# Memory heads first: the order of head pairs in two attention layers of a four-layer kernel

## The chip, the cores and the metric

The kernel runs on one core of a Trainium2 chip. The time is device time in microseconds (us) of one launch. Five engines work side by side, each through its own queue in order: TensorE (PE; its weight loads are listed as PEld), VectorE (DVE), ScalarE (ACT), GpSimd (POOL) and SyncE (SP, which issues the loads). They meet at semaphores.

## What is computed

Two blocks of two layers each. The first block (sliding-window attention with a state-space mixer, then sparse attention) is untouched by the change. In the second block each layer has 12 mixing heads and 4 heads that attend to 256 memory tokens, all 64 wide, over 512 positions; a gated feed-forward network with a short convolution follows. Cut to what matters:

```python
for layer in range(DEPTH):
    xn, mn = rmsnorm(h, norm_mix[layer]), rmsnorm(mem, norm_mem[layer])
    if kind == 0:                      # layer 0: causal, decay by forget gates
        q, k, v, f_logit, qm = jnp.split(xn @ w_in_fox[slot], ...)
        mix = fox_attention(q, k, v, log_sigmoid(f_logit + b_forget))
    else:                              # layer 1: rotary positions, dilated windows
        q, k, v, qm = jnp.split(xn @ w_in_dil[slot], ...)
        mix = dilated_attention(apply_rope(q), apply_rope(k), v)
    mem_out = memory_attention(qm, mn, w_mem_kv[layer])   # softmax(qm km^T / 8) vm
    h = h + merge_heads(concatenate([mix, mem_out])) @ w_out[layer]
    h = h + conv_ffn(rmsnorm(h, norm_ffn[layer]), ...)
```

## The kernel before

All is in fp32. A dense product is made exact enough by splitting both factors into a high and a low part and adding three products (`product`, line 488). The weights come in slots, in the order in which they are listed at lines 419 to 430: SyncE loads a slot, ScalarE or GpSimd copies the high part and GpSimd subtracts for the low part, both on 128x512 pieces, and TensorE uses it. Three slots are kept split at a time; GpSimd begins with the next when TensorE has used up the oldest.

The class `Mixer` (line 2336 on) does attention for one layer. Its heads go in pairs: pairs 0 to 5 are mixing heads, `m0` and `m1` are memory heads. `SEQ` gives the order of the pairs, and each pair has four steps, one for each block `qb` of 128 query rows, so 32 steps. One step is a small pipeline for two heads `e`:

- TensorE `scores`: queries times keys into PSUM bank 0 or 1 (line 2513), in layer 0 with the decay added by a second product from `cum` (line 2521). A mixing pair has 128 (qb + 1) keys, a memory pair always 256. Two steps often share a bank, then the scores of both are issued with the first.
- VectorE `logits`: mask and scale, with a row statistic (line 2676). ScalarE `probs`: exp, with its row sum (line 2630). VectorE `scaled`: reciprocal and multiplication (lines 2685, 2686).
- TensorE `turn`: transposes into banks 2 and 3 (line 2533). ScalarE `copy` brings them to SBUF (line 2640). After a pair's four steps TensorE `values` multiplies with the values into bank 4 (line 2548), and VectorE `finish` splits the result.

Between steps TensorE is fed with the dense products that make the queries, keys and values of later pairs. They are listed as blocks in `self.blocks`, each with its weight slot, kind and bank: "turned" blocks are 512 wide and put queries or keys by head dimension, "tokens" blocks are 256 wide and put values by position. Blocks ahead of `self.prelude` are made before the first step: the first two blocks of queries (banks 4, 5) and of keys (banks 6, 7), in layer 0 the forget gates (bank 0), and the values of pairs 0 and 1, four tiles in banks 1 to 4. The rest stands in `self.fill` and goes between steps, a tokens block or half a turned block in one step, all in banks 6 and 7. ScalarE `evacuate` copies a finished block out of its bank (line 2622). A block may only begin when the block before it in the same bank has been copied.

In layer 1 queries and keys get rotary positions: ScalarE `swap` copies halves crosswise to bank 5 (line 2600), VectorE `rope` multiplies and adds (lines 2700 to 2703). The four tiles of the first pairs are done ahead of the first `logits` on VectorE's queue. In layer 0 VectorE makes the running sum `cum` of the forget gates (lines 2708 to 2717) ahead of it.

TensorE's queue at a start, as the code has it:

```python
for m in range(4, self.prelude):
    self.dense(pe, m, 0, KD)
if layer == 0:
    self.dense(pe, *self.fill[0])
scores(0)
if layer == 1:
    self.dense(pe, *self.fill[0])
for s in range(self.N):
    if s + 1 < self.N:
        scores(s + 1)
    if s + 1 < len(self.fill):
        self.dense(pe, *self.fill[s + 1])
    ...
    turn(s)
```

Of the kernel before, what the change touches and what calls it, by code (L numbers as in the profile page):

```python
# [28 lines left out]
T = S // P  # L29
# [13 lines left out]
FH, FD = 12, 64  # L43
# [298 lines left out]
def block_kernel(nc, t, out):  # L342
    ctx = ExitStack()
    with ctx:
# [8 lines left out]
        def wide(w, c0, width, kd=KD):  # L353

            first = len(W.slots)
            for c in range(c0, c0 + width, 256):
                n = min(256, c0 + width - c)
                W.add(kd, n, [(0, tiles(w, 0, kd)[:, :, c:c + n])])
            return first
# [11 lines left out]
        AW, CW, FW = AH * AD, CH * CD, FH * FD  # L371
# [35 lines left out]
        w_mem_k, w_mem_v, w_q, w_k, w_v, w_qm, w_out = ([0, 0] for _ in range(7))  # L407
# [6 lines left out]
        for layer in range(2):  # L414
            w_in = (fox, dil)[layer]
            w_q[layer], w_k[layer], w_v[layer] = [0] * 3, [0] * 3, [0] * 3
            w_q[layer][0] = wide(w_in, 0, 256)
            w_k[layer][0] = wide(w_in, FW, 256)
            if layer == 0:

                w_forget = wide(w_in, 3 * FW, P)
            w_v[layer][0] = wide(w_in, 2 * FW, 256)
            w_qm[layer] = wide(w_in, 3 * FW + (FH if layer == 0 else 0), 256)
            for i in range(1, 3):
                w_q[layer][i] = wide(w_in, 256 * i, 256)
                w_k[layer][i] = wide(w_in, FW + 256 * i, 256)
                w_v[layer][i] = wide(w_in, 2 * FW + 256 * i, 256)
            w_out[layer] = deep(t["w_out_2"][layer], 0, KD)
            for part, (u0, units) in enumerate(PARTS):
                w_up[layer, part] = len(W.slots)  # L430
                down = tiles(t["w_down_2"][layer], u0, units)
                quarters = {f"{odd + 1}{half + 1}": down[:, odd::2, half * 512:half * 512 + 512] for odd in range(2) for half in range(2)}
                up = tiles(t["w_up_2"][layer], 0, KD)
                for i in range(u0, u0 + units):
                    if i == u0 + units - 2:
                        arrived_12 = W.add_first_quarter(units // 2, quarters["12"])
                    W.add(KD, 256, [(0, up[:, :, i * P:(i + 1) * P]), (P, up[:, :, DFF + i * P:DFF + (i + 1) * P])], i >= SPLIT, part > 0 and i == u0)
                w_down[layer, part] = W.add_group(units // 2, quarters, arrived_12)
# [1899 lines left out]
        class Mixer:  # L2338

            SEQ = (0, 1, "m0", "m1", 2, 3, 4, 5)
            N = 8 * T

            def __init__(self, layer):
# [27 lines left out]
                wq, wk, wv, wqm = w_q[layer], w_k[layer], w_v[layer], w_qm[layer]  # L2373
# [3 lines left out]
                        b.append((slot, "turned", j, bank + j, dst[:, j, :]))  # L2377
                if layer == 0:
                    b.append((w_forget, "forget", 0, 0, None))
                for tile in range(T):  # L2380
                    b.append((wv[0], "tokens", tile, 1 + tile, self.v[:, tile, 0:256]))
                self.prelude = len(b)
                self.first_v = self.prelude - T

                def turned(slot, dst, j0):
                    for j in range(2):
                        b.append((slot, "turned", j, 6 + j, dst[:, j0 + j, :]))

                def tokens(slot, i):
                    for tile in range(T):  # L2390
                        b.append((slot, "tokens", tile, 6 + tile % 2, self.v[:, tile, 256 * i:256 * i + 256]))
                turned(wqm, self.qm, 0)
                turned(wq[1], q_, 2)
                turned(wk[1], k_, 2)
                tokens(wv[1], 1)
# [88 lines left out]
            def tensor(self, pe):  # L2484
                layer, out_ = self.layer, self.out

                def scores(s):
                    i, p, qb = self.steps[s]
                    if self.column(p, qb):
                        return  # L2490
                    if qb == 0:
                        if isinstance(p, str):
                            j = int(p[1])
                            pe.wait_ge(self.evacuated.s, self.evacuated.at(self.made[w_qm[layer], j] + 1))
                            pe.wait_ge(memory.evacuated, 4 * layer + 4)
                        elif layer == 0:
                            pe.wait_ge(self.evacuated.s, self.evacuated.at(self.made[w_k[layer][p // 2], p % 2] + 1))
                        else:
                            place = [(id(d), tile) for d, tile, _ in self.rope_tiles].index((id(self.k), p))
                            pe.wait_ge(self.roped, place + 1)  # L2500
                    if s == 0:
                        pe.wait_ge(self.evacuated.s, self.evacuated.at(self.first_v + 1))
                        if layer == 0:
                            pe.wait_ge(self.cum_ready, 1)
                    else:
                        pe.wait_ge(self.logged.s, self.logged.at(2 * s))
                    decay = layer == 0 and not isinstance(p, str)
                    blocks = (qb, qb + 1) if qb < T - 1 and self.column(p, qb + 1) else (qb,)
                    for b in blocks:
                        c, w = self.column(p, b), self.keys(p, b) * P  # L2510
                        for e in range(2):
                            q_, k_, _ = self.head(p, e)
                            mm = pe.matmul(ps[:, e, c:c + w], q_[:, b * P:(b + 1) * P], k_[:, 0:w], start=b == qb, stop=not decay,  # L2513
                                           skip_group_check=True)
                            if not decay:
                                mm.then_inc(self.scored.s, 1)
                    for b in blocks if decay else ():
                        c, w = self.column(p, b), self.keys(p, b) * P
                        for e in range(2):
                            hd = 2 * p + e  # L2520
                            pe.matmul(ps[:, e, c:c + w], self.sel[:, hd:hd + 1].to_broadcast([LO + FH, P]), self.cum[:, 0:w],  # L2521
                                      start=False, stop=True, skip_group_check=True).then_inc(self.scored.s, 1)

                def turn(s):
                    _, p, qb = self.steps[s]
                    if s == 0:
                        pe.wait_ge(self.evacuated.s, self.evacuated.at(self.first_v + 3))
                    for e in range(2):
                        pe.wait_ge(self.scaled.s, self.scaled.at(2 * s + e + 1))
                        if s >= 1:  # L2530
                            pe.wait_ge(self.copied.s, self.copied.at(2 * (s - 1) + e + 1))
                        for i in range(self.keys(p, qb)):
                            mm = pe.transpose(ps[:, 2 + e, i * P:(i + 1) * P], self.L[:, (2 * s + e) % 4, i * P:(i + 1) * P], ident[:, :])  # L2533
                        mm.then_inc(self.turned.s, 1)
# [58 lines left out]
            def scalar(self, act):  # L2593
                link = linker(act, act_link)

                def swap(i, x):
                    if i >= 1:
                        act.wait_ge(self.swap_free, i)
                    for q in range(4):
                        ins = act.activation(ps[32 * q:32 * q + 32, 5, :], x[32 * (q ^ 1):32 * (q ^ 1) + 32, :], ACT.Copy,  # L2600
                                             scale=1.0 if q % 2 else -1.0)
                    ins.then_inc(self.swapped, 1)
# [21 lines left out]
                def probs(s):  # L2624
                    _, p, qb = self.steps[s]
                    w = self.keys(p, qb) * P
                    for e in range(2):
                        u = (2 * s + e) % 4
                        act.wait_ge(self.logged.s, self.logged.at(2 * s + e + 1))
                        act.activation(self.L[:, u, 0:w], self.L[:, u, 0:w], ACT.Exp, scale=-1.0, bias=self.stat[:, u, 0:1],  # L2630
                                       accum_out=self.stat[:, u, 1:2]).then_inc(self.expd.s, 1)
# [11 lines left out]
                for m in range(self.prelude):  # L2643
                    evacuate(m)
                    if self.layer == 1 and 1 <= m < 5:
                        dst, tile, made = self.rope_tiles[m - 1]
                        act.wait_ge(self.evacuated.s, self.evacuated.at(max(made, 1) + 1))
                        swap(m - 1, dst[:, tile, :])
                probs(0)
                for s in range(self.N):  # L2650
                    if s + 1 < self.N:
# [648 lines left out]
```

## Time and profile before

| | us |
|---|---|
| median of 3 runs | 1711.88 |
| lowest, highest | 1711.48, 1712.64 |
| profiled execution | 1711.19 |
| its span | 1709.4 |
| TensorE busy | 1690.3 (99%) |
| VectorE busy | 1085.2 (63%) |
| GpSimd busy | 915.5 (54%) |
| ScalarE busy | 755.4 (44%) |

The profile is one execution of the program. The mixer of layer 0 lies between about 556 and 740 us, that of layer 1 between about 1136 and 1324 us. TensorE is pipelined: a matmul's record is longer than the distance to the next one's start, so what a group of matmuls costs is read from start to start. "Idle before" in square brackets is the time that the engine sat idle ahead of an instruction, and the arrow names what ended it.

### The profile page before, as it was taken

The numbers are of one execution on the slowest core, as the hardware profiler recorded it, in microseconds if no ns is written. First come the engines' busy times: TensorE is split into PE (matmuls) and PEld (weight loads), VectorE is DVE, ScalarE is ACT, GpSimd is POOL, SyncE is SP. The second block draws the span as 40 slices with busy tenths as digits, with TensorE's granted clock in tenths as the row PEclk, the third lists the DMA queues.
The fourth block names the chain that finished last, engine by engine and source line by source line (L and its number), as shares of the span: only waits on it lengthen the run. The fifth ranks groups of instructions, "written<-read, shape, count | busy, mean of one in ns | idle before, by whom it ended". The sixth has DMA issues, their size and how long they took to land.

```text
span 1709.4 us, 24809 instructions
## 1 busy us (share of the span) xinstructions
PE 1690.3 (99%) x9396; PEld 1368.5 (80%) x9396; DVE 1085.2 (63%) x2179; ACT 755.4 (44%) x1604; POOL 915.5 (54%) x839
## 2 busy tenths in 40 slices
PE   9989999999999999999999999999999999999998
PEld 7866788787689977779888888898777887888886
DVE  6987734796652355534766856866875358477478
ACT  4625523313433344424444444546664345344445
POOL 8524457463347733345654655657344563574474
PEclk9999999999999999999999999999999999999999
DMA  6320323221333321123244144142111323413421
GB/s 187 111 81 24 119 81 105 75 87 62 81 99 96 115 74 50 50 63 95 66 124 123 50 126 121 49 148 97 53 50 50 93 87 105 137 61 102 145 69 55
DMA packets 175102, 152.40 MB, mean 89 GB/s; under 512 B 6224, under 2 KB 149968, under 8 KB 174984
## 3 DMA queue, kind: packets, MB, share of 16 engines
q1 hardware_dynamic: 173384, 149.33, 28.7%
q10 hardware_dynamic: 1600, 1.48, 0.3%
q8 instruction: 75, 1.23, 0.3%
q14 instruction: 43, 0.35, 0.1%
HBM read 147.61 MB, written 2.14 MB: 88 GB/s over the span
## 4 chain that ended last, share of the span: by engine, by line
PE 93%; DVE 4%; ACT 2%; issue 1%; DVEq 0%; ACTq 0%
PE ps L488 77%; PE ps L2513 2%; PE ps L2548 2%; PE ps L2533 2%; PE ps L1970 1%; PE ps L559 1%; PE ps L1948 1%; PE ps L2521 1%; PE ps L1878 1%; PE ps L1041 1%; PE ps L1960 0%; PE ps L1887 0%; PE ps L1048 0%; PE ps L1080 0%; PE ps L991 0%
## 5 line engine op out<-in xcount | busy, mean ns | idle before, releaser
L488 PE MATMUL ps<-x_hi,w_hi 128*128 128x512 f32 (+2 forms) x1432 | 532.2, 372 | 1.0 <-ACT a_gate L1256 0.5
L488 PE MATMUL ps<-x_hi,w_lo 128*128 128x512 f32 (+2 forms) x1432 | 522.5, 365 | 0.0
L488 PE MATMUL ps<-x_lo,w_hi 128*128 128x512 f32 (+2 forms) x1432 | 522.0, 365 | 0.0
L233 POOL TENSOR_SCALAR w_hi<-w_raw 128x512 fp32r<-128x512 f32 x272 | 168.3, 644 | 498.3 <-PE ps L488 477.4
L237 POOL TENSOR_TENSOR w_lo<-w_raw,w_hi 128x512 fp32r<-128x512 f32 x272 | 360.7, 1356 | 5.9
L488 PEld LDWEIGHTS ps<-x_hi,w_hi 128*128 128x128 f32 (+1 forms) x1432 | 269.4, 188 | 60.8 <-issue 16.3
L488 PEld LDWEIGHTS ps<-x_hi,w_lo 128*128 128x128 f32 (+1 forms) x1432 | 269.3, 188 | 44.0
L488 PEld LDWEIGHTS ps<-x_lo,w_hi 128*128 128x128 f32 (+1 forms) x1432 | 269.6, 188 | 40.5
L205 POOL TENSOR_TENSOR w_lo<-w_raw,w_hi 128x512 fp32r<-128x512 f32 x158 | 212.6, 1380 | 139.6 <-ACT w_hi L189 135.8
L2989 DVE SCALAR_TENSOR_TENSOR ffn_cv<-ps,col,ffn_cv 128x510 f32<-128x510 f32 (+1 forms) x176 | 131.8, 749 | 151.9 <-ACT ffn_cv L2933 147.2
L488 PE MATMUL ps<-w_hi,ffn_a_hi 128*128 128x512 f32 x308 | 121.4, 394 | 0.8 <-DVE ffn_a_lo L3010 0.7
L2933 ACT ACTIVATE ffn_cv<-ps,col 128x512 f32<-128x512 f32 x88 | 63.6, 774 | 132.3 <-PE ps L488 132.3
L488 PE MATMUL ps<-w_hi,ffn_a_lo 128*128 128x512 f32 x308 | 120.0, 390 | 0.0
L488 PE MATMUL ps<-w_lo,ffn_a_hi 128*128 128x512 f32 x308 | 120.0, 389 | 0.0
L2630 ACT ACTIVATE mix_L<-mix_L,mix_stat 128x256 f32<-128x256 f32 (+3 forms) x128 | 69.3, 545 | 72.2 <-DVE mix_stat L2676 72.2
L488 PE MATMUL ps<-w_hi,x_hi 128*128 128x256 f32 (+1 forms) x288 | 89.8, 312 | 0.0
L488 PE MATMUL ps<-w_lo,x_hi 128*128 128x256 f32 (+1 forms) x288 | 88.3, 306 | 0.0
L488 PE MATMUL ps<-w_hi,x_lo 128*128 128x256 f32 (+1 forms) x288 | 88.2, 306 | 0.0
L205 POOL TENSOR_TENSOR w_lo<-w_chain,w_hi 128x512 fp32r<-128x512 f32 x44 | 58.8, 1368 | 47.9 <-ACT w_hi L330 47.9
L2686 DVE TENSOR_SCALAR mix_L<-mix_L,mix_stat 128x256 f32<-128x256 f32 (+3 forms) x128 | 80.2, 626 | 4.5
L189 ACT ACTIVATE w_hi<-w_raw 128x512 fp32r<-128x512 f32 x136 | 74.4, 624 | 17.6 <-PE ps L488 14.8
L516 DVE TENSOR_TENSOR h<-h,ps 128x512 f32<-128x512 f32 x32 | 21.8, 687 | 93.8 <-PE ps L488 93.8
(421 smaller groups left out, 2997.9 us busy)
## 6 DMA issues: line engine op xcount, KB each, us to landing
w_raw<-w_up SPq DMA_DIRECT2D x80, 512.0 KB, 5.2
w_raw<-od_w_in SPq DMA_DIRECT2D x12, 1024.0 KB, 5.2
w_raw<-w_in_fox SPq DMA_DIRECT2D x10, 1024.0 KB, 5.4
w_raw<-w_in_dil SPq DMA_DIRECT2D x10, 1024.0 KB, 5.0
w_raw<-w_out SPq DMA_DIRECT2D x8, 1024.0 KB, 5.0
w_raw<-w_down SPq DMA_DIRECT2D x8, 1024.0 KB, 4.9
w_raw<-ev_w_in SPq DMA_DIRECT2D x6, 1024.0 KB, 5.5
w_third<-w_down SPq DMA_DIRECT2D x18, 256.0 KB, 5.2
```

The source lines that it names most:

```text
L189: act.activation(hi, self.piece(r, i), ACT.Copy).then_inc(self.hi_by_act, 1)
L205: ins = pool.tensor_tensor(lo[:, c], self.piece(buffer, i), hi[:, c].bitcast(F32), ALU.subtract)
L233: ins = pool.tensor_scalar(hi[:, c:min(c + PIECE, size)], raw[:, c:min(c + PIECE, size)], 1.0, 1.0, ALU.mult, ALU.mult)
L237: ins = pool.tensor_tensor(lo[:, c:min(c + PIECE, size)], raw[:, c:min(c + PIECE, size)], hi[:, c:min(c + PIECE, size)].bitcast(F32), ALU. ...
L488: mm = pe.matmul(o, l, r, start=start and i == 0, stop=stop and i == 2, skip_group_check=again)
L2513: mm = pe.matmul(ps[:, e, c:c + w], q_[:, b * P:(b + 1) * P], k_[:, 0:w], start=b == qb, stop=not decay, skip_group_check=True)
L2533: mm = pe.transpose(ps[:, 2 + e, i * P:(i + 1) * P], self.L[:, (2 * s + e) % 4, i * P:(i + 1) * P], ident[:, :])
L2548: mm = pe.matmul(ps[64 * e:64 * e + 64, 4, a:S], self.head(p, e)[2](kb), self.PT[:, e, kb, a:S], start=kb == 0, stop=kb == kt - 1, skip_gr ...
L2630: act.activation(self.L[:, u, 0:w], self.L[:, u, 0:w], ACT.Exp, scale=-1.0, bias=self.stat[:, u, 0:1], accum_out=self.stat[:, u, 1:2]).the ...
L2686: dve.tensor_scalar(self.L[:, u, 0:w], self.L[:, u, 0:w], self.stat[:, u, 2:3], None, ALU.mult).then_inc(self.scaled.s, 1)
L2933: act.activation(cv[:, u % 4, half, :], ps[:, self.up_bank(u, half), :], ACT.Identity, scale=self.tap(2, half, u), bias=self.tap(3, half, ...
L2989: ins = dve.scalar_tensor_tensor(o, ps[:, self.up_bank(u, half), 0:S - back], self.tap(j, half, u), o, ALU.mult, ALU.add)
```

## The change

The order of the pairs becomes `m0, m1, 0, 1, 2, 3, 4, 5` in both layers. The two blocks of the memory heads' queries move ahead of the steps, in banks 6 and 7, and the four tiles of the first values move from there (and from banks 1 to 4) into the fill, in banks 6 and 7. The two weight slots change places. The wait of the first scores is rewritten for the new blocks, the wait of the first transposes on the value tiles goes, and ScalarE copies the fill's first block, which is now a whole values tile, ahead of the first exp.

```diff
-            w_v[layer][0] = wide(w_in, 2 * FW, 256)
             w_qm[layer] = wide(w_in, 3 * FW + (FH if layer == 0 else 0), 256)
+            w_v[layer][0] = wide(w_in, 2 * FW, 256)
...
-            SEQ = (0, 1, "m0", "m1", 2, 3, 4, 5)
+            SEQ = ("m0", "m1", 0, 1, 2, 3, 4, 5)
...
-                for tile in range(T):
-                    b.append((wv[0], "tokens", tile, 1 + tile, self.v[:, tile, 0:256]))
-                self.prelude = len(b)
-                self.first_v = self.prelude - T
...
                 turned(wqm, self.qm, 0)
+                self.prelude = len(b)
+                tokens(wv[0], 0)
                 turned(wq[1], q_, 2)
...
                     if s == 0:
-                        pe.wait_ge(self.evacuated.s, self.evacuated.at(self.first_v + 1))
+                        pe.wait_ge(self.evacuated.s, self.evacuated.at(5))
...
                 def turn(s):
                     _, p, qb = self.steps[s]
-                    if s == 0:
-                        pe.wait_ge(self.evacuated.s, self.evacuated.at(self.first_v + 3))
...
+                evacuate(self.fill[0][0])
                 probs(0)
```

What stands on ScalarE's queue at the start of layer 1, from the first dense block of the prelude on. `mix1_v` are values, `mix1_qm` the memory heads' queries, `mix1_k` a key tile whose halves are swapped, `mix1_L` the logits that exp works on. Before:

```order
L2622 ACTIVATE mix1_v_167<-ps 128x256 [waits mix_block]
L2600 ACTIVATE ps<-mix1_k_166 32x512 [waits swap_free,mix_evacuated]
L2600 ACTIVATE ps<-mix1_k_166 32x512 x3
L2622 ACTIVATE mix1_v_167<-ps 128x256 [waits mix_block] x2
L2622 ACTIVATE mix1_v_167<-ps 128x256 [waits w_used]
L2630 ACT_TABLE_LOAD
L2630 ACTIVATE mix1_L_174,mix1_stat_175<-mix1_L_174,mix1_stat_175 128x128 [waits mix_logits] x2
L2630 ACTIVATE mix1_L_174,mix1_stat_175<-mix1_L_174,mix1_stat_175 128x256 [waits mix_logits] x2
```

And in the changed kernel, whose lines have numbers that are 4 smaller there:

```order
L2618 ACTIVATE mix1_qm_168<-ps 128x512 [waits mix_block]
L2596 ACTIVATE ps<-mix1_k_166 32x512 [waits swap_free,mix_evacuated]
L2596 ACTIVATE ps<-mix1_k_166 32x512 x3
L2618 ACTIVATE mix1_qm_168<-ps 128x512 [waits w_used]
L2618 ACTIVATE mix1_v_167<-ps 128x256 [waits mix_block]
L2626 ACT_TABLE_LOAD
L2626 ACTIVATE mix1_L_174,mix1_stat_175<-mix1_L_174,mix1_stat_175 128x256 [waits mix_logits] x4
L2618 ACTIVATE mix1_v_167<-ps 128x256 [waits mix_block]
```

Ahead of the table load that goes with the first exp stand two copies of queries and one of values, where four copies of values stood; the next values tile is copied behind the exps of two steps.

On TensorE's queue the same place in layer 1, only the instructions that wait (each dense block has 24 matmuls, each half block 12; `km` are the memory keys). Before:

```order
L488 MATMUL ps<-w_hi,x_hi 128x256 [waits w_split_done]
L488 MATMUL ps<-w_hi,x_hi 128x256 [waits mix_evacuated]
L2513 MATMUL ps<-mix_k,mix_q 128x128 [waits mix_evacuated,roped]
L488 MATMUL ps<-x_hi,w_hi 128x512 [waits mix_evacuated,w_split_done]
L2533 MATMUL ps<-ident,mix_L 128x128 [waits mix_scaled,mix_evacuated]
```

In the changed kernel:

```order
L488 MATMUL ps<-x_hi,w_hi 128x512 [waits mix_evacuated,w_split_done]
L488 MATMUL ps<-x_hi,w_hi 128x512 [waits mix_evacuated]
L2511 MATMUL ps<-km_127,mix_qm 128x256 [waits mix_evacuated,mem_evacuated]
L488 MATMUL ps<-w_hi,x_hi 128x256 [waits mix_evacuated,w_split_done]
L488 MATMUL ps<-w_hi,x_hi 128x256 [waits mix_evacuated]
L2529 MATMUL ps<-ident,mix_L 128x128 [waits mix_scaled]
L2529 MATMUL ps<-ident,mix_L 128x128 [waits mix_scaled]
L2511 MATMUL ps<-km_127,mix_qm 128x256 [waits mix_logits]
```

The first dense block of the prelude, which waited for its weights alone, now waits for a copy (`mix_evacuated`) as well; the first scores no longer wait for the rotated keys (`roped`); between the first scores and the first transposes stand two tiles of values instead of two halves of a query block.

## Rows read from the trace of the kernel before

**Rows 1.** The page: busy times, and the chain by line.
```profile
PE 1690.3 (99%) x9396; PEld 1368.5 (80%) x9396; DVE 1085.2 (63%) x2179; ACT 755.4 (44%) x1604; POOL 915.5 (54%) x839
...
PE ps L488 77%; PE ps L2513 2%; PE ps L2548 2%; PE ps L2533 2%; PE ps L1970 1%; PE ps L559 1%; PE ps L1948 1%; PE ps L2521 1%; PE ps L1878 1%; PE ps L1041 1%; PE ps L1960 0%; PE ps L1887 0%; PE ps L1048 0%; PE ps L1080 0%; PE ps L991 0%
```

**Rows 2.** TensorE's waits: us in total, times, longest us.
```profile
PE ps L1016 <- DVE s_tmp L1581: 4.9, 1, 4.9
...
PE ps L2513 <- DVE mix_stat L2676: 0.4, 1, 0.4
```

**Rows 3.** Timeline, TensorE, layer 1: start, length, engine, line, operation, tiles.
```profile
1170.63 0.50 PE L488 MATMUL ps<-x_hi,w_hi 128*128 128x512 f32 x1
...
1176.22 0.38 PE L2533 MATMUL ps<-ident,mix_L 128*128 128x128 f32 x2
1176.53 0.92 PE L2513 MATMUL ps<-mix_k,mix_q 64*128 64x384 f32 x4
```

**Rows 4.** Timeline, ScalarE, layer 1.
```profile
1158.36 0.60 ACT L2622 ACTIVATE mix_k<-ps 128x512 f32<-128x512 f32 x1 [2.24 <-PE ps L488]
...
1169.88 0.38 ACT L2622 ACTIVATE mix_v<-ps 128x256 f32<-128x256 f32 x1 [1.46 <-PE ps L488]
1170.28 1.28 ACT L2630 ACT_TABLE_LOAD   x1
1171.59 0.40 ACT L2630 ACTIVATE mix_L<-mix_L,mix_stat 128x128 f32<-128x128 f32 x1
...
1174.02 0.51 ACT L2630 ACTIVATE mix_L<-mix_L,mix_stat 128x256 f32<-128x256 f32 x1 [1.55 <-DVE mix_stat L2676]
```

**Rows 5.** Timeline, VectorE and GpSimd, layer 1.
```profile
1173.66 5.13 POOL L237 TENSOR_TENSOR w_lo<-w_raw,w_hi 128x512 fp32r<-128x512 f32 x4
...
1174.86 1.50 DVE L2686 TENSOR_SCALAR mix_L<-mix_L,mix_stat 128x256 f32<-128x256 f32 x1
...
1176.46 1.17 DVE L2686 TENSOR_SCALAR mix_L<-mix_L,mix_stat 128x256 f32<-128x256 f32 x1
...
1221.25 0.35 DVE L2686 TENSOR_SCALAR mix_L<-mix_L,mix_stat 128x256 f32<-128x256 f32 x1
```

**Rows 6.** TensorE by stretch: length, busy (x), granted clock, DMA share, GB/s.
```profile
1158.25:1169.77 11.52, 11.52 (x97) 1.00 0.27 91
...
572.34:577.81 5.47, 5.47 (x27) 1.00 0.39 108
...
596.32:597.25 0.93, 0.58 (x3) 1.00 0.07 18
...
1227.09:1230.13 3.04, 3.04 (x27) 1.00 0.00 0
1219.31:1222.17 2.86, 2.86 (x15) 1.00 0.00 0
...
1204.51:1205.57 1.06, 1.06 (x9) 1.00 0.00 0
```

**Rows 7.** Timeline, start of layer 0, three engines.
```profile
589.91 1.67 DVE L2717 TENSOR_TENSOR cum<-cum,cum 12x512 fp32r<-12x512 f32 x1
593.89 5.01 POOL L237 TENSOR_TENSOR w_lo<-w_raw,w_hi 128x512 fp32r<-128x512 f32 x4
595.37 1.14 DVE L2686 TENSOR_SCALAR mix_L<-mix_L,mix_stat 128x128 f32<-128x128 f32 x1
596.43 0.41 DVE L2676 CUSTOM_DVE_ANT_0 mix_L<-ps,causal 128x256 f32<-128x256 f32 x1
597.25 0.92 PE L2513 MATMUL ps<-mix_k,mix_q 64*128 64x384 f32 x4 [0.35 <-DVE mix_stat L2676]
```

**Rows 8.** TensorE by stretch, behind its longest wait.
```profile
108.00:110.00 2.00, 1.72 (x8) 0.50 0.93 268
...
108.00:114.00 6.00, 5.72 (x36) 0.60 0.52 172
```

**Rows 9.** Timeline, TensorE's weight loads, layer 1, behind a memory pair's values.
```profile
1232.00 0.42 PEld L2533 LDWEIGHTS ps<-ident,mix_L 128*128 128x128 f32 x4 [0.81 <-DVE mix_L L2686]
```

More of the change, by code:

```diff
@@ L421, in block_kernel @@
                 w_forget = wide(w_in, 3 * FW, P)
+            w_qm[layer] = wide(w_in, 3 * FW + (FH if layer == 0 else 0), 256)
             w_v[layer][0] = wide(w_in, 2 * FW, 256)
-            w_qm[layer] = wide(w_in, 3 * FW + (FH if layer == 0 else 0), 256)
             for i in range(1, 3):
```

## The prediction, made before the changed kernel was run

> **What bounds the kernel now.** I read the page's busy times and the chain that ended last first: TensorE is busy 99% of the span, and of the chain 77% of the span lie in the one line that all its dense products share [rows 1]. A change here pays only by what it does to TensorE's own queue: it can take a wait of that engine away or add one. The list of TensorE's waits is then the budget for a gain. Its longest entries belong to the first block, and of the two layers with memory heads it holds one wait of 0.4 us [rows 2]. The timeline is sharper, because a matmul's modelled end hides a short gap: in layer 0 the first transposes start at 596.32 and the next scores at 597.25, 0.93 us later, where the same two transposes in layer 1 take from 1176.22 to 1176.53, 0.31 us [rows 3, 6, 7]. So 0.62 us are lost at the start of layer 0, and nothing is at the start of layer 1, where fills, transposes and scores follow without a gap. Little is there to be won. I therefore looked at what the change puts in front of TensorE at the two starts.
>
> **Work that only moves.** Both orders issue the same matmuls. The prelude loses four value tiles, 11.52 us, and gets two blocks of the memory queries, twice the forget block's 5.47 us, 10.94 us [rows 6]. The fill between steps changes the other way: a values tile takes 3.04 us from start to start behind another fill, half a query block 2.86 us [rows 6], so four fills cost about 0.6 us more (0.18 x 4 is 0.7). Gain and loss cancel; I count zero, at most 0.2 us either way. The scores, transposes and value products come in another order at the same price. Loads and weight splits keep their shape and their places in the queues of SP and GpSimd (the two swapped weight slots have one size). The memory keys that the first scores now need are made in an earlier stage. All this costs nothing.
>
> **Layer 1, first new wait: the bank.** Value tile 0 went to bank 1, which was free. The query block goes to bank 6, which still holds the first half of the keys. Both halves of the keys end together at 1158.25, where the value tiles now start [rows 3]; ScalarE copies the first half from 1158.36 for 0.60 us [rows 4]. TensorE can begin at 1159.02: +0.77 us. The second half is copied while the first query block runs, 5.47 us: no wait. In layer 0 the forget block lies between and covers both copies, so nothing is added there.
>
> **Layer 1, second new wait: exp behind a values tile.** This is the term that decides. ScalarE works in order. Before, its last copy of the prelude ends and its table load begins at 1170.28, and the first exp runs at 1171.59, while TensorE has two whole fills, 1170.63 to 1176.22, before it wants a transposed result [rows 3, 4]. Now ScalarE must first copy value tile 0, and TensorE makes that tile only behind the first scores. Step by step: query blocks end at 1159.02 + 10.94 = 1169.96; scores of two memory steps take 1.06 us [rows 6], to 1171.02; tile 0 ends 2.88 us (a quarter of 11.52) later, 1173.90. The copy starts 0.11 later, the load 0.40 after that, exp 1.31 after the load began, all as in [rows 4]: exp starts at 1175.72 and not at 1171.6. From a 256-wide exp's start to the start of its scaling it was 0.84 us (1174.02 to 1174.86 [rows 4, 5]), so the first scaling begins at 1176.56. GpSimd is then in the middle of the subtractions that end at 1178.79 [rows 5]. Scalings of this width take 0.35 us beside an idle GpSimd and 1.17 to 1.50 us beside these subtractions [rows 5]; the one that began at 1176.46 ended at 1177.63. I take that row for the first and the end of GpSimd's batch for the second, 1178.9. The next logits take 0.82 us until TensorE may overwrite their bank (596.43 to 597.25 [rows 7]), so the third step's scores start at 1179.7. TensorE alone would be there at 1176.78 (second fill) + 0.62 (four transposes, twice the 0.31) = 1177.4. Wait: 2.3 us. With no contention the scalings end at 1176.9 and 1177.45, the scores start at 1178.3, and the wait is 0.9 us. Layer 1 costs 0.77 + 2.3 = 3.1 us, with ends at 1.7 and, should the batch stand 0.8 us later, 4.0.
>
> The Trainium skill, GPSIMD Engine Reference, section Key points, says that GpSimd shares its SBUF interfaces with VectorE, with contention for VectorE instructions in a two-port mode or with two SBUF inputs. By that rule the scaling suffers and the logits, which read PSUM, don't. The trace agrees: the 128x256 logits took 0.41 us inside GpSimd's batch [rows 7].
>
> **Layer 0.** The fill of tile 0 already stands ahead of the first scores, so the copy is early: forget ends at 577.81, 10.94 + 2.88 later it is 591.63. The running sum of the forget gates is ready at 591.58 [rows 7]: no wait, but no margin. The exp table is loaded 0.5 us after the tile, to 593.47, just as the first logits are ready (scores 1.06 us, logits 0.41 us). The first scaling falls at 594.3, again into the GpSimd batch from 593.89 to 598.90, as before [rows 7]. So both scalings end where they ended, the second at 596.51, and the next scores start at 597.25 again. But TensorE has less to do until then: 591.63 + 1.06 + 2.88 + 0.62 = 596.19. The wait is 1.06 us where it was 0.62: +0.4 us, from -0.6 (no contention) to +1.8 (one subtraction more, 5.01 / 4 = 1.25 us).
>
> **Later steps.** In layer 1 the rope tiles of the second queries and keys now fall beside the second memory pair and pair 0. A memory pair needs half as many value products, and every second memory step has no scores, so VectorE has less cover in steps 5 to 9; in return the later ropes get more. Before, TensorE's weight loads waited 0.81 us once behind a memory pair's values [rows 9], and its matmuls not at all by the list. I add 0.2 us, between -0.3 and +1.
>
> **The sum.** 3.1 + 0.4 + 0.2 = +3.7 us. The profiled execution took 1711.19 us (its span is 1709.4, 1.8 lie around it), so it would take 1714.9; the median of three is 1711.88, so I predict 1715.6.
>
> **Rivals.** *The scalings miss GpSimd's batch.* The price falls to 1.7 in layer 1 and to about -0.6 in layer 0; with one of the four scalings still caught it is more: +1.1 to +2.9, time 1713.0 to 1714.8. For it: the batch's position moves with every rope before it. Against it: the batch starts at 1173.66, behind a batch that GpSimd finishes without waiting, and the change leaves those alone. It decides from where the two scalings together wait less than 1.5 us. This one is not slower by the bound.
> *The clock.* After the longest wait of the kernel, 4.9 us, the granted clock was 0.50, the lower of its two levels (1.2 against 2.4 GHz), and over the 6 us from 108 to 114 it averaged 0.60 [rows 2, 8]: 6 x 0.40 = 2.4 us lost. If layer 1's waits (0.8 before the first scaled tile, 1.3 before the second, the rest ahead of the scores) bring that about, the time is 1711.9 + 3.7 + 2.4 = 1718.0. Against it: transposes lie between, and the 0.62 us of layer 0 left the clock at 1.00 [rows 6]. The Trainium skill, TensorE: Matmul & The Clock Gate, section Part 1: The HAM clock gate, says that an idle array falls to half clock; by that rule, too, the total wait would have to be one stretch.
> *The ropes are the gain.* If TensorE loses more beside ropes than starts show, say the 0.81 us [rows 9] and as much again in steps that I can't see, and the table load is hidden after all, the change saves 1.5 to 2 us: 1710. To be faster by 3.4 us it would need more idle time than both layers have.
> That the change does something else than it says is ruled out by the order of instructions.
>
> **Chances.** Forecast, +3.0 to +4.8: 0.56, of which 0.45 lie above 3.4 us. Missed batch: 0.27. Clock or a like addition: 0.08. Ropes: 0.09, of which 0.04 faster. A measurement of this kernel can tell about 0.2%, 3.4 us, from no change; the forecast lies just above it. Slower 0.45 + 0.08 = 0.53, same 0.11 + 0.27 + 0.05 = 0.43, faster 0.04. The range takes in the missed batch and the clock: 1713.0 to 1718.1 (rounded out).
>
> **What would show it.** In the profile after: in layer 1 a TensorE gap of 0.7 to 0.8 us between the key block and the queries' block; ScalarE's copy of a values tile and the table load ahead of layer 1's first exp, which runs about 4.1 us later than before; first transposes of layer 1 waiting on the scaling, then scores waiting on the logits, together 2.3 us; scalings of 1.1 to 1.3 us there; in layer 0 the same scores at 597.25. I am wrong if exp runs before the values copy, if the scalings take 0.35 us, or if the waits are there and the span does not grow by their sum, which would mean that gaps I did not see were closed elsewhere.

## The result, and the profile after

The changed kernel is slower: a median of 1717.49 us (1716.89 to 1718.48) against 1712.03 us for the kernel before on the same chip, a ratio of 1.0031 with a 95% interval of 1.0020 to 1.0042. That is +5.5 us, where 1715.6 us, +3.7, had been forecast; the range, up to 1718.1, held it. The profiled execution took 1717.48 us, its span is 1715.7 (before 1709.4).

TensorE's busy time on the page is the same as in [rows 1] to 0.1 us, so no work came on; it waits more. Engine, busy us, share, instructions:

```profile
PE 1690.4 (99%) x9396; PEld 1368.5 (80%) x9396; DVE 1082.4 (63%) x2179; ACT 755.8 (44%) x1604; POOL 917.9 (53%) x839
```

The list of TensorE's waits in layer 1 (1136 to 1324 us), where before there was none (us in total, times, longest):

```profile
PE ps L2529 <- DVE mix_L L2683: 1.3, 2, 0.8
PE ps L488 <- ACT mix_k L2618: 0.8, 1, 0.8
PE ps L2511 <- DVE mix_stat L2673: 0.7, 3, 0.3
PE ps L2529 <- ACT mix_PT L2636: 0.3, 1, 0.3
```

The timeline of TensorE shows the places. The first row is the query block that waits for its bank, then come the first scores, the transposes of the first step (two and two) and the third step's scores, which answer to [rows 3]; the last row is the last transposes of layer 1.

```profile
1160.35 0.47 PE L488 MATMUL ps<-x_hi,w_hi 128*128 128x512 f32 x1 [0.78 <-ACT mix_k L2618]
...
1171.40 1.13 PE L2511 MATMUL ps<-km,mix_qm 64*128 64x256 f32 x8
...
1178.90 0.44 PE L2529 MATMUL ps<-ident,mix_L 128*128 128x128 f32 x2 [0.42 <-DVE mix_L L2683]
...
1180.17 0.44 PE L2529 MATMUL ps<-ident,mix_L 128*128 128x128 f32 x2 [0.83 <-DVE mix_L L2683]
...
1180.86 1.13 PE L2511 MATMUL ps<-km,mix_qm 64*128 64x256 f32 x8 [0.25 <-DVE mix_stat L2673]
...
1318.86 1.03 PE L2529 MATMUL ps<-ident,mix_L 128*128 128x128 f32 x8
```

ScalarE, same place, against [rows 4]: the values copy and the table load stand ahead of the first exp, which starts at 1177.34 instead of 1171.59.

```profile
1159.61 0.60 ACT L2618 ACTIVATE mix_k<-ps 128x512 f32<-128x512 f32 x1 [2.23 <-PE ps L488]
...
1175.64 0.38 ACT L2618 ACTIVATE mix_v<-ps 128x256 f32<-128x256 f32 x1 [3.53 <-PE ps L488]
1176.04 1.28 ACT L2626 ACT_TABLE_LOAD   x1
1177.34 0.51 ACT L2626 ACTIVATE mix_L<-mix_L,mix_stat 128x256 f32<-128x256 f32 x1
```

The Trainium skill, ScalarE: Activation LUTs, section What ACT_TABLE_LOAD costs, gives 1283 ns for the load, as here, and adds a drain of about 1380 ns. The trace shows no such drain in this place: exp starts 1.30 us behind the load's start.

VectorE and GpSimd, same place, against [rows 5]: two scalings beside GpSimd's four subtractions (last row), and one after them.

```profile
1178.17 0.68 DVE L2683 TENSOR_SCALAR mix_L<-mix_L,mix_stat 128x256 f32<-128x256 f32 x1
...
1178.95 1.17 DVE L2683 TENSOR_SCALAR mix_L<-mix_L,mix_stat 128x256 f32<-128x256 f32 x1
...
1181.33 0.35 DVE L2683 TENSOR_SCALAR mix_L<-mix_L,mix_stat 128x256 f32<-128x256 f32 x1
...
1174.91 5.05 POOL L237 TENSOR_TENSOR w_lo<-w_raw,w_hi 128x512 fp32r<-128x512 f32 x4
```

Layer 0, TensorE, against [rows 7]: first transposes and third step's scores.

```profile
596.45 0.38 PE L2529 MATMUL ps<-ident,mix_L 128*128 128x128 f32 x2
...
597.38 0.44 PE L2529 MATMUL ps<-ident,mix_L 128*128 128x128 f32 x2 [0.55 <-DVE mix_L L2683]
...
598.06 1.13 PE L2511 MATMUL ps<-km,mix_qm 64*128 64x256 f32 x8 [0.25 <-DVE mix_stat L2673]
```

**How the runs are read.** The time of day of a row differs between executions by what came before it. Inside the two mixers the distance between two rows does not: it repeats to 0.03 us between executions of one kernel (e10 and e11 below). So each kernel is read by three marks. In layer 0 the distance from the start of the forget block to the start of the last transposes (before 168.81 us, after 169.25). In layer 1 two pieces, *start*, from the end of the key block (0.21 us behind the start of its last matmul) to the third step's scores, and *rest*, from there to the last transposes. For the changed kernel the key block ends at 1159.50, so start is 1180.86 - 1159.50 = 21.36, and rest 1318.86 - 1180.86 = 138.00. Differences from the kernel before (168.81, 18.28, 136.91), with the medians against the kernel before in the same job (1712.03, 1711.96, 1712.01 and 1711.65 us):

| kernel | layer 0 | layer 1 start | layer 1 rest | sum | median |
|---|---|---|---|---|---|
| changed kernel | +0.44 | +3.08 | +1.09 | +4.61 | +5.46 |
| e1 layer 0 only | +0.41 | 0.00 | 0.00 | +0.41 | +0.27 |
| e2 exp first | +0.44 | +1.06 | +1.11 | +2.61 | +2.74 |
| e3 banks 2, 3 | +0.44 | +1.82 | +1.09 | +3.35 | +3.76 |
| e4 table early | +0.43 | +1.82 | +1.07 | +3.32 | +3.33 |
| e5 short batch | +0.47 | +1.97 | +1.10 | +3.54 | +3.36 |
| e6 exp first, banks | +0.43 | +0.07 | +1.11 | +1.61 | +1.93 |
| e7 e6, other order | +0.45 | +0.07 | -0.26 | +0.26 | +0.43 |
| e8 layer 0 scores first | -0.70 | -0.01 | 0.00 | -0.71 | -0.57 |
| e9 both | -0.70 | +0.07 | -0.26 | -0.89 | -0.34 |

The intervals of the medians are about 0.1% (1.7 us) to each side. The sums, worked out from one profile each, follow the medians to 0.9 us. The medians alone would not tell neighbours apart.

### The profile page after: what moved, and what is told of

It is laid out like the page before. It is cut to its first block, busy times and chain, and to the rows that moved or that the text cites. A ratio compares the mean times of both kernels' runs of the same rounds, so it can differ in the third digit from the quotient of the medians.

```text
span 1715.7 us, 24808 instructions
## 1 busy us (share of the span) xinstructions
PE 1690.4 (99%) x9396; PEld 1368.5 (80%) x9396; DVE 1082.4 (63%) x2179; ACT 755.8 (44%) x1604; POOL 917.9 (53%) x839
## 4 chain that ended last, share of the span: by engine, by line
PE 84%; DVE 8%; ACT 3%; POOL 2%; DMA 1%; issue 1%; SPq 0%; DVEq 0%; ACTq 0%
PE ps L488 71%; PE ps L2511 2%; PE ps L2544 2%; PE ps L2529 2%; POOL w_lo L205 1%; PE ps L1970 1%; PE ps L559 1%; PE ps L1948 1%; DVE ps L1587 1%; DVE ffn_cv L2986 1%; PE ps L2519 1%; DMA w_chain<-w_down 1%; PE ps L1878 1%; PE ps L1960 0%; PE ps L1887 0%
```

## The experiments

All diffs are against the changed kernel and cut to what matters; three dots mark what is left out.

**One layer alone (e1).** Layer 1 keeps the old order, blocks and slots.

```diff
+                if layer == 1:
+                    self.SEQ = (0, 1, "m0", "m1", 2, 3, 4, 5)
...
```

> The changed order in layer 0 only; layer 1 as in the kernel before. My theory (layer 1 pays at its start and beside its ropes, layer 0 pays 0.4 us at its start): layer 0's mixer about 0.4 us longer than before, layer 1's mixer as before (158.9 us from the end of the key block to the values of the last but one pair), median within 1 us of the kernel before. Rival (the order costs something in the rest of the program, the feed-forward layers or the weight splits): 1 us or more of the change's 5.5 us stays.

Measured: 1712.23 us, ratio 1.0002 [0.9992, 1.0011]. Layer 0 has the +0.41 us of the changed kernel, layer 1 none of its loss. So the two layers add up, and layer 1 has nine tenths of it.

**Exp ahead of the values copy (e2).** The table load and the first exps need the scores alone, so they can run before ScalarE waits for the values tile.

```diff
-                evacuate(self.fill[0][0])
                 probs(0)
+                evacuate(self.fill[0][0])
```

> The changed kernel with ScalarE's two calls swapped: the exps of step 0 stand ahead of the copy of the first values tile, in both layers. If the copy is what delays the first exp in layer 1: exp starts about 1.3 us after the copy of the second query block and not 5.8 us after it as in the changed kernel, TensorE waits for neither the first scalings nor the next logits, and the third step's scores come 1.9 us earlier in layer 1; in layer 0 0 to 0.6 us. Sum -1.9 to -2.5 us. Rival (GpSimd's batch or the ropes hold the scalings back whatever stands on ScalarE): less than 1 us.

Measured: 1714.70 us, ratio 1.0015 [1.0006, 1.0025]. In the timeline of ScalarE (first rows) the first exp starts right behind the load, in that of TensorE (last rows) scores follow the transposes without a wait, 0.53 us later:

```profile
1171.49 1.28 ACT L2626 ACT_TABLE_LOAD   x1
1172.79 0.51 ACT L2626 ACTIVATE mix_L<-mix_L,mix_stat 128x256 f32<-128x256 f32 x1
...
1175.01 0.38 ACT L2618 ACTIVATE mix_v<-ps 128x256 f32<-128x256 f32 x1 [1.12 <-PE ps L488]
...
1177.68 0.60 PE L2529 MATMUL ps<-ident,mix_L 128*128 128x128 f32 x4
1178.21 1.13 PE L2511 MATMUL ps<-km,mix_qm 64*128 64x256 f32 x8
```

Start falls from +3.08 to +1.06: the order of this one copy costs 2.02 us. In layer 0 it gains nothing (+0.44, as in the changed kernel): the values tile is made before the first scores there, so exp is not held up by it.

**The bank (e3).** Layer 1's query blocks go to banks 2 and 3, which are free.

```diff
+                    bank = 2 if layer == 1 and slot == wqm else 6
...
-                        b.append((slot, "turned", j, 6 + j, dst[:, j0 + j, :]))
+                        b.append((slot, "turned", j, bank + j, dst[:, j0 + j, :]))
```

> The changed kernel with layer 1's memory queries in PSUM banks 2 and 3, free at that point, instead of 6 and 7. If the bank wait is a cost of its own: the gap between key block and query block (0.85 us) goes and the third step's scores come 0.85 us earlier. Rival (GpSimd's batch sets when the scalings end, and it does not move with TensorE): the gap goes, but the scalings end where they ended, the wait for them grows by as much, and the gain at the third step's scores is under 0.3 us.

Measured: 1715.72 us, ratio 1.0022 [1.0013, 1.0032]. The first scores come 1.00 us earlier (10.90 instead of 11.90 us behind the keys), but the third step's scores 1.26 us earlier.

**The table early (e4).** A one-element exp ahead of the copy pulls the table load forward; the copy stays ahead of the real exps.

```diff
+                link(act.activation(seam_stat[:, 0, 0:1], eps_col[:, 0:1], ACT.Exp))
                 evacuate(self.fill[0][0])
```

> The changed kernel with one tiny exp on a column ahead of the copy of the first values tile, so that the table load is done while TensorE makes the tile. It measures the load's share. If exp's start sets the wait: exp 1.28 us earlier in layer 1, the third step's scores 1.2 to 1.3 us earlier; in layer 0 0 to 0.6. Rival (the wait is set by GpSimd's batch alone): exp is earlier, the scores are not.

Measured: 1715.29 us, ratio 1.0021 [1.0012, 1.0031]. Exp comes 1.3 us earlier, start falls by 1.26 us. That e3 and e4 gain the same 1.26 us by edits of different size is told by e4's timeline, VectorE's scalings and GpSimd's batch:

```profile
1176.20 0.77 DVE L2684 TENSOR_SCALAR mix_L<-mix_L,mix_stat 128x256 f32<-128x256 f32 x1
...
1177.07 1.19 DVE L2684 TENSOR_SCALAR mix_L<-mix_L,mix_stat 128x256 f32<-128x256 f32 x1
...
1174.27 5.12 POOL L237 TENSOR_TENSOR w_lo<-w_raw,w_hi 128x512 fp32r<-128x512 f32 x4
```

A quarter of 5.12 is 1.28, so GpSimd's four subtractions end near 1175.55, 1176.83, 1178.11 and 1179.39. The scalings end at 1176.97 and 1178.26, each 0.15 behind one of them. In the changed kernel the ends are 1178.85 and 1180.12, again 0.15 behind 1178.70 and 1179.96. These are not four lucky rows: in each of the thirteen profiles, every one of the 38 to 41 scalings of both mixers that began beside one of these subtractions ended 0.08 to 0.16 us behind the end of one. So what such a scaling gains goes in steps of a subtraction, 1.26 us here.

**A shorter batch (e5).** GpSimd leaves out three of the four subtractions of one key slot of layer 1, the four that the scalings meet; three quarters of its low part then stay as they were. All else is the changed kernel's.

```diff
-        for c in range(0, size, PIECE):
+        for c in range(size - PIECE if n == self.short else 0, size, PIECE):
...
+            W.short = w_k[1][1] if layer == 1 else None
```

> The changed kernel, but GpSimd leaves out three of the four subtractions for the low part of one weight slot of layer 1 (the second keys block), those of the batch that runs beside the first scalings; the low part is left as it was, nothing else changes. If GpSimd's batch stretches the scalings: they take 0.35 us each, the third step's scores stand about 20.3 us behind the end of the key block and not 21.36 (-1.0 us), and the rest of the mixer is as long as in the changed kernel (138.0 us from there to the last transposes). Rival (ScalarE's late exp alone): under 0.3 us.

Measured: 1715.37 us, ratio 1.0019 [1.0010, 1.0029]. The timeline has GpSimd's one subtraction, which ends at 1175.95, and VectorE's scalings behind it, 0.35 us each:

```profile
1174.66 1.29 POOL L237 TENSOR_TENSOR w_lo<-w_raw,w_hi 128x512 fp32r<-128x512 f32 x1
...
1177.90 0.35 DVE L2684 TENSOR_SCALAR mix_L<-mix_L,mix_stat 128x256 f32<-128x256 f32 x1
...
1178.39 0.35 DVE L2684 TENSOR_SCALAR mix_L<-mix_L,mix_stat 128x256 f32<-128x256 f32 x1
```

Start falls by 1.11 us, to +1.97. As GpSimd's batch is all that changed, it is shown to be what stretched the scalings. The remaining wait is that of e5 over e2, 1.97 - 1.06 = 0.91 us. So the 2.02 us of the copy's place are 0.91 for the late exp and 1.11 for the batch it then meets.

**Both repairs (e6).** Exp first and banks 2 and 3.

> The changed kernel with both repairs at once: exps of step 0 ahead of the values copy, and layer 1's memory queries in banks 2 and 3. Together they should take away all of the start's cost in layer 1: third step's scores 18.3 us behind the key block as in the kernel before (-3.0 us against the changed kernel), and leave 1.1 us that arise in steps 9 to 11. Median about 1.5 to 2 us above the kernel before. Rival (the repairs overlap, since GpSimd's batch gave one of them its 1.26 us): 0.5 us or more is left at the start.

Measured: 1713.94 us, ratio 1.0011 [1.0002, 1.0020]. Start is +0.07, so the work that moved does cancel, and the bank costs 1.06 - 0.07 = 0.99 us. But rest stays at +1.11, as in e2 to e5: this loss has nothing to do with the start.

**The order of pairs (e7).** e6 with pair 0 between the memory pairs in layer 1, so that steps 8 to 11, beside which the second keys are rotated, are a memory pair's.

```diff
+                if layer == 1:
+                    self.SEQ = ("m0", 0, "m1", 1, 2, 3, 4, 5)
```

> As the run with both repairs, but layer 1 takes the pairs in the order m0, 0, m1, 1, 2, 3, 4, 5, so that the ropes of steps 9 and 11 stand beside a memory pair again and those of steps 5 and 7 beside pair 0. If the 1.1 us come from wide softmax steps beside the ropes of steps 9 and 11, right behind a memory pair's short steps: they go, the mixer of layer 1 is within 0.2 us of the kernel before (155.2 us to the last transposes). Rival (any wide pair beside a rope pays): 0.5 us or more stays, now in steps 5 to 7.

Measured: 1712.44 us, ratio 1.0003 [0.9994, 1.0013]; rest falls from +1.11 to -0.26, and TensorE has no wait listed in layer 1. The loss is thus bound to the order of the pairs, and e7's rival fell: pair 0 stands beside tiles in steps 5 and 7 there and waits nowhere. In the changed kernel steps 8 to 11 are pair 0's, and TensorE's rows show where they lose:

```profile
1215.57 0.92 PE L2511 MATMUL ps<-mix_k,mix_q 64*128 64x384 f32 x4 [0.19 <-DVE mix_stat L2673]
...
1225.09 0.93 PE L2511 MATMUL ps<-mix_k,mix_q 64*128 64x128 f32 x8 [0.26 <-DVE mix_stat L2673]
...
1229.35 1.06 PE L2529 MATMUL ps<-ident,mix_L 128*128 128x128 f32 x8 [0.28 <-ACT mix_PT L2636]
```

Measured from start to start, the four steps from 1214.94 lose 0.26 us ahead of the first of these scores, 0.27 in the fill behind them, 0.32 ahead of the second scores and 0.43 in the fill ahead of the last transposes, 1.28 in all. Rest shows 1.09 of it, since without waits it is a little shorter than before (e7: -0.26). The first two losses fall in step 9, the others in step 11. ScalarE's timeline, around that last wait:

```profile
1224.37 0.72 ACT L2626 ACTIVATE mix_L<-mix_L,mix_stat 128x512 f32<-128x512 f32 x1 [3.07 <-DVE mix_stat L2673]
...
1225.91 2.29 ACT L2596 ACTIVATE ps<-ps 32x512 f32<-32x512 f32 x4
1228.23 0.60 ACT L2618 ACTIVATE mix_k<-ps 128x512 f32<-128x512 f32 x1
1228.72 0.87 ACT L2636 ACTIVATE mix_PT<-ps 128x384 f32<-128x384 f32 x2
```

The copy of the transposes, for which the next transposes wait, stands behind two 512-wide exps, four halves swapped for the rotation (2.29 us) and the block's copy. In front of that, VectorE's timeline: it rotates a key tile, finishes the memory pair and scales before it comes to the 512-wide logits for which the scores at 1225.09 wait.

```profile
1219.33 0.69 DVE L2697 TENSOR_TENSOR rope_tmp<-ps,rope_sin 128x512 f32<-128x512 f32 x1 [1.51 <-ACT mix_k L2618]
...
1221.98 0.69 DVE L2690 TENSOR_TENSOR mix_m_lo<-ps,mix_m_hi 128x512 fp32r<-128x512 f32 x1
...
1224.25 0.69 DVE L2673 CUSTOM_DVE_ANT_0 mix_L<-ps,dilated_mask 128x512 f32<-128x512 f32 x1
```

A memory pair has 256-wide steps there, 0.42 us of logits in place of 0.69, and its scores come for two steps at once.

Width alone is not the whole of it, since pair 0 in e7 and pair 1 in the kernel before pass steps 4 to 7 without a wait. The changed kernel's VectorE comes late into step 9: it rotates the second query tile and scales step 8 beside a batch of GpSimd's, in the last row.

```profile
1209.77 1.75 DVE L2698 TENSOR_TENSOR mix_q<-mix_q,rope_cos 128x512 f32<-128x512 f32 x1
1211.56 1.66 DVE L2700 TENSOR_TENSOR mix_q<-mix_q,rope_tmp 128x512 f32<-128x512 f32 x1
...
1213.32 1.11 DVE L2683 TENSOR_SCALAR mix_L<-mix_L,mix_stat 128x128 f32<-128x128 f32 x1
...
1208.41 5.93 POOL L237 TENSOR_TENSOR w_lo<-w_raw,w_hi 128x512 fp32r<-128x512 f32 x4
```

Away from GpSimd the same two instructions take 0.68 and 0.69 us for a key tile (at 1219.94 and 1220.66). In the kernel before, this tile's rotation and the scalings behind it are stretched as well, but TensorE still has a mixing pair's transposes, and its value products take 2.31 us from start to start where a memory pair's take 1.87; step 9's logits end 0.9 us before TensorE is at step 8's transposes, where here they end 0.6 us behind that point. How the 1.28 us divide between this late entry and the wide steps is read from the timelines alone; no run separates them.

**Layer 0's scores first (e8).** Layer 1 is as before the change; in layer 0 the first scores go ahead of the fill, exp ahead of the values copy, and the wait for `cum` moves to the first mixing pair, which the new order allows.

```diff
-                        if layer == 0:
-                            pe.wait_ge(self.cum_ready, 1)
...
-                if layer == 0:
-                    self.dense(pe, *self.fill[0])
                 scores(0)
-                if layer == 1:
-                    self.dense(pe, *self.fill[0])
+                self.dense(pe, *self.fill[0])
...
```

> Layer 1 as in the kernel before. Layer 0 in the changed order, but its first scores stand ahead of the first values tile and do not wait for the running sum of the forget gates, which memory heads don't need; that wait stands at the scores of pair 0. If layer 0's wait at the start is the chain of logits, exp and scaling behind one fill only: two fills cover it and layer 0 is 0.6 us shorter than in the kernel before (168.2 us from the forget block to the last transposes, against 168.81), median 0.6 us below it, which the timing alone cannot tell. Rival (the sum of the forget gates on VectorE holds the first logits back as long): no gain, 168.8 to 169.3 us.

Measured: 1711.44 us, ratio 0.9997 [0.9987, 1.0007]. Layer 0 takes 168.11 us, 0.70 less than before and 1.14 less than the changed kernel: the first transposes (at 595.89) and the next scores (at 596.42) stand 0.53 us apart, without a wait. That is the 0.62 us of the old wait and little more.

**The best of both (e9).** e7's layer 1 and e8's layer 0.

> Layer 0 as in the run that put the first scores ahead of the fill (last transposes 168.11 us behind the start of the forget block, before 168.81), layer 1 as in the run with the order m0, 0, m1, 1, banks 2 and 3 and exp ahead of the copy (155.00 us behind the end of the keys, before 155.19). If the two gains add and nothing is lost behind them: -0.70 - 0.19 = -0.9 us against the kernel before, a median of about 1711.1, ratio 0.9995. The rival is that the second feed-forward network gives part of it back, as it did in the changed kernel and in the run with layer 0's scores first, where the stretch behind layer 1 took 396.8 us instead of 396.0: then the two cancel, 1712.0, ratio 1.0000.

Measured: 1711.31 us against 1711.65, ratio 0.9997 [0.9988, 1.0006]. The mixers give -0.89 us by the traces; the medians can't tell that from nothing. The rival did not come: the stretch behind layer 1 took 1709.0 - 1313.07 = 395.9 us.

**Both kernels again (e10, e11).** No edit; one more profile of each.

> The changed kernel itself, profiled a second time. The stretches inside the two mixers should repeat to 0.03 us: last transposes at 169.25 us in layer 0 and 159.36 us in layer 1. The question is the 0.9 us behind layer 1 (396.84 us from the last transposes to the end of the span, 395.96 before) and the 0.7 us ahead of layer 0 (573.04 against 572.34). If they belong to the change they come again within 0.1 us; if they belong to one execution, the landing times of its loads above all, they differ by 0.3 us or more.

> The kernel before, profiled a second time, for the same question: 168.81 us and 155.19 us inside the mixers again; the stretch ahead of layer 0 (572.34) and the one behind layer 1 (395.96) repeat within 0.1 us if they belong to the kernel, and move by 0.3 us or more if they belong to one execution.

Measured: 1717.55 and 1711.03 us. The mixers repeat (169.22 and 159.37; 168.79 and 155.18). Outside them the changed kernel took again more than the kernel before: ahead of layer 0 573.15 and 572.35 us (first profiles 573.04 and 572.34), behind layer 1 396.4 and 395.9 (396.8 and 396.0). Between the mixers it was 417.7 and 416.9 (417.2 and 417.1). So the stretch ahead of layer 0 came again within about 0.1 us, while the one behind layer 1 moved by 0.5 in the changed kernel: in part it belongs to one execution.

## Why the prediction was right, and where it was off

**The number:** right in part by luck. Its own case was +3.0 to +4.8 us. The mixers, where its terms lie, gave +4.61, but the median gave +5.46, above that case; the range held it only because it had been widened to 1718.1 for the clock, which stayed at full speed.

**What moved costs nothing:** right. e6 has all of it and a start of +0.07 us; in e7, where no wait is left, layer 1 as a whole is 0.19 us shorter than before, within the 0.2 allowed.

**The bank:** right in kind, a little small. Forecast 0.77, the row says 0.78, the net price by e6 against e2 is 0.99.

**Exp behind the values tile:** right, step by step. Forecast 2.3 us, 0.9 of it without contention; e2 and e5 give 2.02 and 0.91. Less the 1.25 us by which the changed kernel's layer 1 began later, the first scaling started at 1176.92 (forecast 1176.56), the second ended at 1178.87 (1178.9), the scores started at 1179.61 (1179.7). Exp was 0.4 us later than forecast, because bank and query blocks took 0.2 us more than forecast, and scores and tile another 0.2; GpSimd's boundary took that up. The start as a whole was forecast at 3.1 and measured at 3.08; the bank's surplus and the wait's deficit cancel.

**Layer 0:** right. The gap from first transposes to next scores is 1.61 us, of which 0.53 are the four transposes: 1.08 us of waiting, forecast 1.06. e1 gives +0.41, forecast +0.4.

**Later steps:** the term that was mis-sized. Forecast +0.2 us between -0.3 and +1, measured +1.09. The mechanism it named, less cover for VectorE in steps 5 to 9 behind a memory pair with half as many value products, fits the 0.53 us of step 9. But it was only put in words: no row of VectorE's queue was set against what TensorE has to do there. The 0.75 us of step 11 lie where it forecast a gain ("the later ropes get more"): the tiles of the second keys stand beside pair 0, whose steps ask more of VectorE and ScalarE as they get wider, while TensorE's fill does not grow.

**What no step named:** the mixers account for 4.61 of the 5.46 us; 0.85 are left, within the interval. The two first profiles differ by more, 6.3 us of span; of the other 1.7 us, 0.9 lie behind layer 1 and 0.7 ahead of layer 0. Behind layer 1 the profiles have two waits that are new, in TensorE's timeline:

```profile
1554.73 0.50 PE L488 MATMUL ps<-w_hi,ffn_a_hi 128*128 128x512 f32 x1 [0.39 <-POOL w_lo L205]
...
1680.76 0.50 PE L488 MATMUL ps<-w_hi,ffn_a_hi 128*128 128x512 f32 x1 [0.41 <-POOL w_lo L205]
```

Ahead of each stands a 1 MB load of `w_chain` from `w_down`. The first, issued at 1542.88, in the view by tile, from issue to landing:

```profile
DMA to landing us min/median/max: 5.3/5.3/5.3
```

ScalarE's and GpSimd's halves of that weight, and then TensorE, follow its landing at once. It took 4.9 and 5.0 us in the two profiles of the kernel before and 5.3 and 5.4 in those of the changed kernel; over all thirteen profiles, 4.8 to 5.1 us in those with at most 396.0 us behind layer 1, 5.2 to 5.4 in those with more. The second load, issued at 1668.89, took 5.3 to 5.4 us and made its wait in three profiles (the changed kernel's first, e3 and e8, 396.8 to 396.9 us behind layer 1), and 4.8 to 4.9 us without one in the other ten. Why the loads are slower in some executions is open.

Ahead of layer 0 both kernels issue the same, yet one wait is there that the kernel before does not have, in the first block:

```profile
142.50 0.70 PE L1147 MATMUL ps<-a_k,a_q 64*128 64x256 f32 x4 [1.60 <-DVE soft_stat L1651]
...
138.91 1.58 DVE L1598 TENSOR_TENSOR s_X<-s_X,s_tmp 128x512 f32<-128x512 f32 x1
...
135.73 5.90 POOL L237 TENSOR_TENSOR w_lo<-w_raw,w_hi 128x512 fp32r<-128x512 f32 x4
```

TensorE was 1.0 us ahead of its time before at this place, so GpSimd's batch, for which it sets the start, came 1.2 us earlier (before at 136.97) and met more of VectorE's work (the row at L1598 took 1.04 us before); VectorE was 0.7 us later and TensorE lost more than it had been ahead. That is the same meeting as at layer 1's start, read from two traces and tested by no run. Five of the thirteen profiles have this wait at 1.1 to 1.6 us, with 573.0 to 573.5 us ahead of layer 0; the others have it at 0.14 or less, and at most 572.7 us. Why TensorE was ahead is open.

**The rivals.** *Missed batch* fell: neither scaling took 0.35 us, and both ended with a subtraction. *The clock* fell: the mean granted clock stayed at 1.00 over the waits of layer 1's start and over both mixers (TensorE by stretch, columns as in [rows 6]).

```profile
1171.40:1180.86 9.46, 7.95 (x62) 1.00 0.33 111
...
556.00:1330.00 774.00, 769.14 (x4188) 1.00 0.27 83
```

*The ropes are the gain* fell with its sign turned: the ropes beside pair 0 cost 1.1 us. That the likeliest case was put at 0.2 for them, and this rival at a gain, was one error made twice.

**Small slips in the sums,** none of which changes the forecast: 2.3 us and a batch 0.8 us later make 3.9 us for layer 1 and not 4.0; 0.4 and 1.25 make +1.7 for layer 0 and not +1.8; and 1158.25 stands in [rows 6], not in [rows 3].

## What to carry to other kernels

At a seam, place the copy that an in-order engine can only do late behind the work that it can do at once: one line's place cost 2.0 us here. When pairs of unlike width change places, sum each engine's work per step, not only the engine that is full, and look at how late the others come into a step: wide steps beside extra tiles cost 1.1 us in steps 8 to 11 and nothing in steps 4 to 7. Where an instruction of one engine ends only with one of another engine's batch, as VectorE's scalings did here, a wait for it moves in whole instructions of that batch, so a repair of 1.0 us and one of 1.3 us were worth the same.

## What the runs showed of the chip

A scaling on VectorE that began beside one of GpSimd's 128x512 subtractions ended 0.08 to 0.16 us behind the end of one of them, in all 38 to 41 cases of each of the thirteen profiles. At 128x256 it took 0.35 us alone and 0.42 (e3) to 1.50 us beside them. The Trainium skill, GPSIMD Engine Reference, section Key points, names the contention; these rows, with e3 and e4, show its size here and that it goes by whole instructions. Also not expected: stretches inside a mixer repeat to 0.03 us between executions of one kernel, while the same 1 MB load took between 4.8 and 5.4 us.
